# Expert groups of 32 tokens in four 32-column strips, the down product one group late

## The reference, cut to what matters

```python
# router: top 4 of 32 experts for each of 256 tokens, softmax over the four
hgu  = tok[rows] @ w_gu[e] + b_gu[e]              # 1024 -> 2048
gate = minimum(hgu[:, 0::2], 7.0)
up   = clip(hgu[:, 1::2], -7.0, 7.0)
act  = (up + 1.0) * (gate * sigmoid(1.702 * gate))
y    = (act @ w_down[e] + b_down[e]) * wts        # 1024 -> 1024
out[row_tok] += y
```

```
22 47 28 13 13 19 39 88 40 103 26 14 36 25 15 51
17 30 18 64 20 25 61 27 63 25 20 26 11 17 12  9
```

## Time and profile before

| | |
|---|---|
| median of 3 runs | 1385.5 us (1385.05 to 1386.11) |
| profiled execution, span | 1383.6 us |
| TensorE busy | 1307.4 us, 94% |
| moved by DMA | 455.91 MB, mean 330 GB/s |

### The profile page before, as it was taken

One profiled execution on the slowest core, in us unless ns is written; L12 is line 12 of the kernel. 1 busy time (PEld: TensorE's weight loads), 2 busy tenths in 40 slices (PEclk: granted clock), 3 DMA queues, 4 the chain that ended last, 5 costly groups with the idle time before them and its releaser, 6 DMA issues.

```text
span 1383.6 us, 15858 instructions
## 1 busy us (share of the span) xinstructions
PE 1307.4 (94%) x6029; PEld 613.6 (44%) x6030; DVE 281.6 (20%) x831; ACT 250.2 (18%) x514; POOL 18.5 (1%) x26
## 2 busy tenths in 40 slices
PE   8999999999889999999999999999999999999998
PEld 4664858886443333333343333333333333333332
DVE  3234333651410111101111112011110110111011
ACT  2124421460111111110111101111011110111101
POOL 1100000000000000000000000000000000000000
PEclk9999999999889999999999999999999999999999
DMA  9942355223687999986938999999999999999991
GB/s 335 316 151 73 111 196 197 94 81 122 257 356 319 427 427 426 427 340 265 425 160 369 425 427 427 427 426 423 426 426 428 426 425 425 425 427 427 426 423 69
DMA packets 66261, 455.91 MB, mean 330 GB/s; under 512 B 7284, under 2 KB 13016, under 8 KB 33432
## 3 DMA queue, kind: packets, MB, share of 16 engines
q1 hardware_dynamic: 65528, 454.13, 79.8%
q0 software_dynamic: 256, 0.79, 0.2%
q10 hardware_dynamic: 448, 0.60, 0.1%
HBM read 454.45 MB, written 1.05 MB: 329 GB/s over the span
## 4 chain that ended last, share of the span: by engine, by line
PE 78%; DMA 17%; ACT 2%; DVE 1%; issue 1%; ACTq 0%; SPq 0%; DVEq 0%
PE bank L1007 25%; DMA ring<-in_w_down 17%; PE bank L1037 15%; PE bank L555 6%; PE bank L695 6%; PE bank L978 4%; PE bank L994 3%; PE bank L970 3%; PE bank L604 2%; PE bank L891 2%; PE bank L857 2%; PE bank L544 1%; PE bank L1026 1%; ACT mq L1303 1%; PE bank L581 1%
## 5 line engine op out<-in xcount | busy, mean ns | idle before, releaser
L1007 PE MATMUL bank<-ring,sp_ 128*64 128x512 f32 x2176 | 479.9, 599 | 0.0
L1007 PEld LDWEIGHTS bank<-ring,sp_ 128*64 128x64 f32 x2176 | 154.4, 138 | 324.0 <-issue 324.0
L1037 PE MATMUL bank<-ring,mq 128*64 128x512 f32 x1088 | 245.7, 601 | 35.6 <-ACT mq L1303 23.7
L1037 PEld LDWEIGHTS bank<-ring,mq 128*64 128x64 f32 x1088 | 76.7, 138 | 181.3 <-issue 153.7
L1735 DVE TENSOR_SCALAR sp_<-bank 128x256 f32<-128x256 f32 x68 | 28.5, 420 | 572.2 <-PE bank L1007 572.2
L1299 ACT ACTIVATE sp_<-sp_ 128x256 f32<-128x256 f32 x68 | 28.3, 416 | 509.2 <-DVE sp_ L1735 509.2
L555 PE MATMUL bank<-ring 128*128 128x512 f32 x192 | 83.2, 592 | 0.0
L1751 DVE TENSOR_SCALAR sp_<-cst,rank_it,w_it 128x64 f32<-128x64 f32 x68 | 16.7, 311 | 280.2 <-PE bank L1007 280.2
L695 PE MATMUL bank<-ring 128*128 128x256 f32 x320 | 71.3, 381 | 0.0
L970 PEld LDWEIGHTS bank<-sp_,sc 128*128 128x128 f32 x544 | 64.5, 198 | 15.2 <-issue 15.2
L994 PE MATMUL bank<-bg,cst 1*64 1x512 f32 x272 | 66.9, 609 | 3.8 <-issue 3.8
(11 more groups left out here) (293 smaller groups left out, 839.9 us busy)
## 6 DMA issues: line engine op xcount, KB each, us to landing
ring<-in_w_gu SPq DMA_DIRECT2D x128, 2048.0 KB, 25.1
ring<-in_w_down SPq DMA_DIRECT2D x64, 2048.0 KB, 16.5
ring<-in_w_in SPq DMA_DIRECT2D x13, 2048.0 KB, 10.4
ring<-in_w_out SPq DMA_DIRECT2D x2, 2048.0 KB, 8.5
ring<-in_w_mem_kv SPq DMA_DIRECT2D x2, 1024.0 KB, 7.4
ring<-in_w_mem_kv SPq DMA_DIRECT2D x1, 2048.0 KB, 8.0
ring<-in_cmp_w_k SPq DMA_DIRECT2D x1, 2048.0 KB, 8.5
ring<-in_cmp_w_v SPq DMA_DIRECT2D x1, 2048.0 KB, 8.5
```

Source lines behind the costliest of these rows:

```text
L1007: mm = nc.tensor.matmul(BH[b][64 * hh:64 * hh + 64, :], xgT[:, k, 64 * par:64 * par + 64], w[:, c, o:o + 512], start=False, stop=k == KT - ...
L1037: mm = nc.tensor.matmul(BG[64 * hh:64 * hh + 64, :], actT[:, o:o + 64], w[:, c, 512 * hh:512 * hh + 512], start=k == 0, stop=k == KT - 1, ...
```

## The change

`SLOT_TOK` goes from 64 to 32. A group fills 32 stationary columns, and four matmuls with different weight columns write the four 32-partition strips of one bank. The down product splits its contraction over two strips for each half of the output columns, and the scatter sums them, since the weighted one-hot holds each token twice. The activation has half as many elements per item and one instruction of each kind. The gather moves 64 columns for a pair instead of 128. The order becomes: up(2j), down(2j-1), scatter, up(2j+1), down(2j), gather. The item list may hold 64 entries; for an odd number of items the last pair has an empty item that is computed all the same.

```diff
-SLOT_TOK = 64
+SLOT_TOK = 32
@@ SP
-            load_round(1, True, [0, 1, 2, 3, 4, 5])
             steady = [0, 1, 4, 5, 2, 3]
+            load_round(1, True, steady)
@@ PE, gate/up part q
-                        for b in range(2):
-                            for hh in range(2):
-                                o = 1024 * b + 512 * hh
-                                mm = nc.tensor.matmul(BH[b][64 * hh:64 * hh + 64, :], xgT[:, k, 64 * par:64 * par + 64],
-                                                      w[:, c, o:o + 512], start=False, stop=k == KT - 1,
+                    for s in range(4):
+                        mm = nc.tensor.matmul(BH[par][32 * s:32 * s + 32, :], xgT[:, k, 32 * par:32 * par + 32],
+                                              w[:, c, 512 * s:512 * s + 512], start=k == 0, stop=k == KT - 1,
@@ PE, down
+                    for c in range(2):
+                        for two in range(2):
+                            o = P * two + 32 * (2 * d + c)
+                            for hh in range(2):
+                                mm = nc.tensor.matmul(BG[64 * hh + 32 * two:64 * hh + 32 * two + 32, :], actT[par][:, o:o + 32],
+                                                      w[:, 2 * c + two, 512 * hh:512 * hh + 512],
+                                                      start=d + c == 0, stop=d + c == 2, skip_group_check=True)
@@ PE, a pair of items
+            def pair(j, first=False, final=False):
+
+                i0, i1 = j * 2, j * 2 + 1
+                e0, e1 = [item(bass.ds(j * 2 + (NE + par), 1), NE - 1) for par in range(2)]
+                odd0, odd1 = [item(bass.ds(j * 2 + (NE + ITEMS + par), 1), 1) for par in range(2)]
+                if not first:
+                    before_e = item(bass.ds(j * 2 + (NE - 1), 1), NE - 1)
+
+                def left(row):
+                    pe.wait_ge(S("g_evac"), j * 2 + 1)
+                    up(0, e0, 0, row)
+                    bias(0, row)
+                    up(1, e0, 0, row)
+                    pe.wait_ge(S("g_evac"), j * 2 + 2)
+                    up(2, e0, 0, row)
+                    up(3, e0, 0, row)
+                    if not first:
+                        turn(j * 2 - 1, 1, j)
+                        down(j * 2 - 1, before_e, 1)
+
+                def right(row):
+                    up(0, e1, 1, row)
+                    bias(1, row)
+                    up(1, e1, 1, row)
+                    up(2, e1, 1, row)
+                    up(3, e1, 1, row)
+                    if not final:
+                        turn(i0, 0)
+                        down(i0, e0, 0)
+
+                either(odd0, left)
+                if not first:
+                    pe.wait_ge(S("y_evac"), j * 2)
+                    pe.wait_ge(S("st_evac"), j)
+                    scatter()
+                either(odd1, right)
+                if not final:
+                    pe.wait_ge(S("G_ready"), j + 2)
+                    pe.wait_ge(S("y_evac"), j * 2 + 1)
+                    gather()
@@ PE, after the last pair
+            pair(last_pair, final=True)
+            turn(last_pair * 2, 0)
+            down(last_pair * 2, e0, 0)
+            turn(last_pair * 2 + 1, 1, last_pair + 1)
+            pe.wait_ge(S("y_evac"), last_pair * 2 + 1)
+            down(last_pair * 2 + 1, e1, 1)
@@ ACT, results of an item
+            def results(i, par, scattered=None):
+
                 act.wait_ge(S("a_full"), i + 1)
-                nc.scalar.activation(actT, BX[:, :], ACT.Copy).then_inc(S("a_evac"), 1)
+                nc.scalar.activation(actT[par], BX[:, 0:256], ACT.Copy).then_inc(S("a_evac"), 1)
+                if scattered is not None:
+                    act.wait_ge(S("scattered"), scattered)
+                if par:
+                    nc.scalar.activation(STs, BX[:, 256:512], ACT.Copy).then_inc(S("st_evac"), 1)
                 act.wait_ge(S("down_done"), i * 2 + 2)
                 nc.scalar.activation(y_sb[64 * par:64 * par + 64, 0:512], BG[0:64, :], ACT.Copy)
                 nc.scalar.activation(y_sb[64 * par:64 * par + 64, 512:1024], BG[64:P, :], ACT.Copy).then_inc(S("y_evac"), 1)
```

More of the change, by code:

```diff
@@ L1021, in down, with bias @@
[L1021 to L1026, removed]
+            def bias(par, row):
+                p = 32 + 32 * row
+                for s in range(4):
+                    mm = nc.tensor.matmul(BH[par][32 * s:32 * s + 32, :], ones[p:p + 1, 0:32], brow[row][:, 512 * s:512 * s + 512],
+                                          start=False, stop=False, skip_group_check=True)
+                mm.then_inc(S("brow_used"), 1)
@@ L1027, in down @@
                 mm.then_inc(S("a_full"), 1)
+            def down(i, e, par):
                 pe.wait_ge(S("a_evac"), i + 1)
@@ L1031, in down @@
                     w = ring[:, 4 + d, :].rearrange("p (c n) -> p c n", c=4)
[L1032 to L1039, removed]
@@ L1040, in down @@
-                    mm.then_inc(S("down_done"), 1)
[L1042 to L1055, removed]
+                    for c in range(2):
+                        for two in range(2):
+                            o = P * two + 32 * (2 * d + c)
[3 more added lines that the diff above has]
+                                                      start=d + c == 0, stop=d + c == 2, skip_group_check=True)
@@ new lines, in down, with item, either @@
+                    mm.then_inc(S("down_done"), 1)
+            def item(at, most):
+                return pe.value_load(idx[0:1, at], min_val=0, max_val=most)
+            def either(odd, work):
+                with pe.If(odd > 0):
+                    work(1)
+                with pe.Else():
+                    work(0)
+            def pair(j, first=False, final=False):
[30 more added lines that the diff above has]
+                either(odd1, right)
@@ L1066, in pair @@
[L1066 to L1073, removed]
             pe.wait_ge(S("G_ready"), 1)
@@ L1079, in _ @@
             last_pair = pe.value_load(idx[0:1, NE + 2 * ITEMS:], min_val=NE // 2 - 1, max_val=ITEMS // 2 - 1)
-            with pe.Fori(0, last_pair) as j:
+            pair(0, first=True)
+            with pe.Fori(1, last_pair) as j:
                 pair(j)
-            pair(last_pair, final=True)
+            pe.wait_ge(S("bdn_in"), 16)
+            for i in range(NT):
+                for hh in range(2):
+                    nc.tensor.matmul(ACC[i][hh][:, :], rTs[:, 256 + P * i:256 + P * i + P],
+                                     b_dn[:, 512 * hh:512 * hh + 512], start=False, stop=False, skip_group_check=True)
+            pair(last_pair, final=True)
+            e0, e1 = [item(bass.ds(last_pair * 2 + (NE + par), 1), NE - 1) for par in range(2)]
+            turn(last_pair * 2, 0)
[3 more added lines that the diff above has]
+            down(last_pair * 2 + 1, e1, 1)
             pe.wait_ge(S("last_y"), 1)
@@ L1683, in _ @@
             step(V.tensor_scalar(rk, rk, UNSEL, None, ALU.add))
-            for n in range(3):
-                ins = V.tensor_scalar(cntc[:, n:n + 1], bank("rank")[0:NE, 64:65], float(SLOT_TOK * (n + 1)), None, ALU.is_gt)
-            step_read(ins, "rank")
+            step(V.tensor_copy(count, bank("rank")[0:NE, 64:65]))
+            step_read(V.tensor_scalar(cntc, C("full")[0:NE, :], count, None, ALU.is_lt), "rank")
             step(V.tensor_reduce(nit, cntc, AX.X, ALU.add))
@@ L1760, in _ @@
             last_pair = dve.value_load(idx[0:1, NE + 2 * ITEMS:], min_val=NE // 2 - 1, max_val=ITEMS // 2 - 1)
-            with dve.Fori(0, last_pair + 1) as j:
+            pair(0, first=True)
+            with dve.Fori(1, last_pair) as j:
                 pair(j)
+            pair(last_pair, final=True)
             for t in range(NT):
```

186 lines of the change are left out of this document (89 added, 97 removed).

## The result

The changed kernel takes 1509.2 us, median of four runs (1504.2 to 1512.19), against 1385.62: 1.0893 times the time of before, 95% interval 1.0868 to 1.0917. The profiled execution has a span of 1506.7 us, 123.1 above before. Forecast were 1459 and a range up to 1500: the sign is right, the size is not.

What follows compares the result with a forecast made beforehand. TensorE was taken to bound until expert 9 is done, transfers after. Expert 10's down chunks start at 775.2, L(11) is 795.1, twenty experts (598) plus 23 lost give 1416; the tail brings a 1458 span, 1459 median, range 1415 to 1500.

Steps and rivals of the forecast that it cites:

- Four strips share a step: TensorE matmuls: four records in four strips take one step of 0.429 us, so gate/up is 8.2 and down 3.66.
- that rival: TensorE packing: four strips are worse than a step, matmul steps a quarter longer, about 1535 us; chance 0.08.
- Single experts: Experts with one item: transfers bound them at 29.9 us each, and their down slots come free without loss.
- L(6): Landing of chunk 3, the last gate/up chunk, of expert 6; forecast at 561.1 us. Other numbers mean other experts.
- five small dips: Transfer rate behind expert 10: dips of 4 to 5 us at the five twofold experts 12, 15, 19, 22, 24.
- the sum of 37.7: TensorE's time for a pair of items: products, transposes, copies, scatter, gather and bare reads, 37.7 us or 18.85 an item.
- 1.9 us stay bare: Head of a pair: instruction passing and five `idx` reads outlast the 3.78 us gather, leaving TensorE idle 1.9 us.
- tail: From the last expert's last gate/up chunk to the span's end: 39 us, plus about 3 for lower clock and late landings.
- the loss of a twofold expert: Late stage, experts with two items: down slots come free too late, about 4.6 us lost each.
- the prediction's own formula: Twofold experts' down slots: free 4.9 us plus two items after landing, start 1.8 later, wanted 39.9; loss about 4.6 us.
- c: TensorE's time for one item, forecast at 18.85 us; the late stage stays untouched only up to 16.6.
- The rival with the half clock: Single experts' waits: TensorE idles a third of the time, clock halves, 12 to 25 us more, 1475 to 1485; chance 0.2.

Runs made afterwards that it cites:

- e1: Changed kernel with the register reads of `idx` moved from the head of a pair to behind the scatter and the down product; 1462.45 us, 1.0601 times before.
- e4: Changed kernel with the gather's halves put into other banks, so that it no longer waits for the copies of the down result; 1498.19 us.
- e7: Changed kernel with both repairs, `idx` reads moved behind the scatter and the gather in other banks, order kept; 1435.15 us, single run.
- e6: Changed kernel with groups of 32 kept, but the order of the kernel before and the `idx` reads behind the scatter; 1408.83 us, 1.0167 times before.
- e2: Changed kernel with four more reads of the item list, values unused, at the head of each pair; 1559.65 us, single run.

## Why the prediction was wrong

**What held.** Four strips share a step: the 48 records of three parts take 5.29 us, 12 steps of 0.441 with the changes of block. The Trainium skill, "TensorE: Matmul & The Clock Gate", Part 3, has a measured 2.38 times for three column tiles; the trace doesn't agree with it for four strips of 512 float32 columns, which ran at four to a step wherever the clock was full, and that rival is out. Up 8.13 (forecast 8.2), down 3.68 (3.66), copies 1.27 (1.35) at two places of a pair, scatter 3.70 (3.63), gather 3.80 (3.78) though it moves half the columns. Single experts still take 29.8 us (L(3) to L(6): 474.63 to 564.07, against 29.9). A late issue for expert 10, six slices of dips ahead of it, five small dips behind it, and the order of the stages came as described, the delay and the small dips larger than forecast. And e1, where a pair takes 37.15, ends at a span of 1459.1; the forecast was 1458 from a pair of 37.7. The step from the pair to the end is thus about right, though its pair is made up differently: no bare reads, and a clock that falls in two pairs of five.

**What failed** is the head of a pair in the sum of 37.7. Its term "1.9 us stay bare" measured 2.55 on average, 0.65 more. The larger part is something that the sum had nowhere: the first part wholly or mostly at 1.2 GHz, 2.85 to 3.64 instead of 1.85 us in each of the five pairs, and in three of them the bias and the rest as well (1.86 and 6.7 for 0.99 and 5.29), together 2.85 us a pair. A pair was 41.26 for 37.7. The sum priced every step behind the pause at the full clock and gave no reason for it. The prediction had seen a low clock behind a pause, but it looked for it only in single experts, where TensorE idles a third of the time, and gave it 12 to 25 us there. The low clock is there as well and delays the release of the slots, which the table below has as x; but it costs more where TensorE is the bound.

How 48.7 us come out of it:

| term | forecast | measured | us |
|---|---|---|---|
| L(6) | 561.1 | 564.07 | 3.0 |
| last part to the issue of the down chunks, x | 4.9 | 6.84 | 1.9 |
| 11 items of experts 6 to 9 | 11 x 18.85 | 11 x 20.63 | 19.6 |
| rest up to expert 10's issue (773.4, 799.66) | | | 1.8 |
| issue to L(11) | 21.7 | 821.83 - 799.66 = 22.17 | 0.5 |
| L(11) to L(31) | 621 | 1467.03 - 821.83 = 645.2 | 24.2 |
| tail | 42 | 39.7 | -2.3 |

Behind L(11), the loss of a twofold expert was put at 4.6 us, 23 for five; it is 47.9 (from the landing ahead of each to the one behind it, less 59.8: 9.6, 9.6, 11.9, 9.3 and 7.5). By the prediction's own formula with measured terms, slots are free at x + 2c = 6.84 + 41.26 = 48.1, the start is at 49.9, wanted 39.9: 10.0 us each, and 9.6 measured on average. So the formula was right on average, and both of its terms were too small: c, since the head of a pair was priced too low, and x, since the last part of a product runs at half clock behind its wait for weights (3.64 for 1.85). With 11 items in the cluster and five twofold experts, c brings 1.78 x (11 + 10) = 37 us by the formula, and x brings six times 1.9, some 12. The rival with the half clock had the second, smaller one (it put x at 8.9), and not the first.

**Where the 123.1 us come from**, by spans of the runs: the reads at the head and the clock behind them 1506.7 - 1459.1 = 47.6; the copies ahead of the gather and the rest of the low clock 1459.1 - 1433.3 = 25.8; the late order itself, with the reads moved in both, 1433.3 - 1412.2 = 21.1; and with everything of that undone, 45 groups for 34 are left: 1412.2 - 1383.6 = 28.6. The split depends on the order in which the edits are undone, as e1, e4 and e7 show, and e7 is a single run. Of the last part, 741.95 - 729.47 = 12.5 us lie ahead of expert 10's issue and 16.1 behind it. It stays open how much of it is the clock, which in e6 is at 0.86 from 800 to 1340, where before has 0.99.

## What to carry to other kernels

Where the end hangs on when buffers come free, count from the landing to the release, and let every wait in between have its price in the stage in which TensorE is the bound; here a microsecond in a pair was worth 12 to 13. Registers that a loop needs are best read ahead of a block that waits for nothing new, not at the head of the loop behind a short one, and a wait for a result just made wants other work in front of it. Smaller groups pay only if an item shrinks by more than the number of items grows: here 11 for 6 asked for 15.4 us, and the best was 16.7.

## What the runs showed of the hardware

- Two pauses as short as 1.27 and 2.5 to 2.65 us around a gather of 3.80 are followed by the clock at 0.50, for some 3.6 us in two of five pairs and for 7 to 8 in three (1.86 and 6.7 for 0.99 and 5.29). The one ahead of the gather alone is enough in three heads of six (e1), the one behind it in five of six (e4); with neither the clock stays at 1.00 (e7).
- The same 1.27 us stand ahead of the scatter, and there the clock did not fall: it takes 3.70 us and the part behind it 1.85 in every pair of this stage, in the kernel after and in e1 to e4. So the length of a pause doesn't decide alone. What sets the gather apart (its records move 64 columns, the scatter's 512) was not tested.
- TensorE's sequencer comes to the register reads behind a block only when it has passed the block's instructions on: in the kernel after they begin 2.1 us behind the release of the gather. In e1 three of them run from 659.8 to 661.3 under a scatter that ends at 663.35, and cost nothing. A read takes 0.30 us by its record, and four more were 2.6 us more of bare time (e2), 0.65 each.
- Half the moving columns do not make the gather faster: 32 records, each with a weight load of 128 columns, take 3.80 us with 64 moving columns and 3.78 with 128. That the weight loads set this pace is likely, but no run changes them.
- A queue that had run dry needs 22.17 us from the issue to the landing of four chunks of 2 MB, 2.3 more than the 19.9 that they take in a full one.
